# Hybrid decoder step on one core: 14 of 17 tiles of h reach the router through a DRAM round trip and VectorE's 32x32 transposes

## Chip, core and metric

One core of one Trainium2 chip runs one launch of the kernel. The metric is the time of that launch on the device in microseconds (us), lower is better. All arrays are float32. Engines are named as the profile names them: PE is TensorE (PEld its weight loads), DVE is VectorE, ACT is ScalarE, POOL is GpSimd, SP is SyncE, here the engine that issues most DMAs.

## What is computed

One decoder layer for 2048 prompt tokens and 8 sample tokens, model width 1024:

```python
proj = x @ w_in + b_in                      # attention and convolution halves side by side
attn = window_attention(rope(q), rope(k), v)   # window 128, 8 heads, 2 kv heads
conv = silu(layer_norm(depthwise_conv(ca * sigmoid(cg)))) 
mix  = concat(attn, conv) @ w_out + b_out
h    = layer_norm(ALPHA * x + mix)          # (2056, 1024)
lg, le = h @ w_rg, h @ w_re                 # router: 4 groups, 32 experts
# top-1 group, top-2 experts in it, gates; every token goes to 2 SwiGLU experts
y    = layer_norm(ALPHA * h + moe(h))
```

The change concerns only how `h` is brought into the layout in which the router's product `h @ [w_rg, w_re]` reads it: model dimension on partitions, tokens on columns.

## The kernel before

The program has five stages: the input projection of the convolution half; attention with the rest of the input projection; the **output sweep**; the expert loop; the final LayerNorm. Each engine has its own instruction stream, and the streams meet at semaphores (`after(engine, sem, c)` waits for the count c + 1).

The output sweep handles one tile per step `c` = 0 to 16 (`OUT_IN`: first the sample tile of 8 rows, then the 16 prompt tiles of 128 rows). It runs as a software pipeline, and every engine has a hand-written order:

- **PE**, step c: `project_out(c, 0)` (L850, 8 products of 512 columns, the first half of h's columns), `turn_z(c+1)` (L830, four transposes of the convolution output), `router(c-2)` (L868, 8 small products of hT with the router weights), `project_out(c, 1)`, `rank(c-2)` (L875, L876), and `turn_h(c-1)` (L859): 8 transposes of 128x128, which read `r[:, k::8]` and write the PSUM tile `bank_T`.
- **ACT**: `turned_h` (L1151) copies `bank_T` into `hT` in SBUF, one instruction, and raises `hT_ev`. `router(c)` waits for `hT_ev`; it also waits for `rk_ev`, which DVE's `route_count` of the tile before raises.
- **DVE**, step c: `route_count(c-3)` and `route_slot(c-3)` (L1554 to L1564), `conv_stats(c+2)` (L1450, waits for the tile of `conv_rows`), `gain_conv(c+1)` (L1458), `add_half(c, 0)` (L1483), `route_top(c-2)` (L1507 to L1534), `mix_conv(c+1)` (L1466), `route_gate(c-2)` (L1540 to L1549), `add_half(c, 1)` (L1483, raises `o1_ev`), `norm_h(c)` (L1490 to L1495).
- **POOL and ACT** finish h (`rstd_h`, `scale_h`, `bias_h`), which raises `h_ok`.
- **SP**, step c: `load_conv(c+2)` (L503), `store_h(c-1)` (L528 to `h_rows`, L529 to `sum_rows`, 512 KB each), `load_attn(c+2)` (L512, waits for PE's second half), `load_x(c+2)` (L522, waits for `o1_ev` of c), and for c = 1 to 9 `load_matrix` (L489): 1 MB of expert weights each, ahead of the expert loop.

`h` is stored to DRAM (`h_rows`) for every tile in any case, since the expert loop gathers its rows from there. `hT` has one buffer (the old `ptA`); `ptB` (`flat_ptB`) is free during the sweep.

Of the kernel before, what the change touches and what calls it, by code (L numbers as in the profile page):

```python
# [14 lines left out]
P = 128  # L15
# [142 lines left out]
pe_o0 pe_o1 o0_ev o1_ev lstat_ok lrs_ok dg_ok lz_ok h_ok h_out0 h_out1 pe_hT hT_ev pe_ro ro_ev ro_nm ro_e1 ro_d ro_e2  # L158
oh_ok pe_rk rk_ev slot_ok sc_out0 sc_out1 last_out s_cache s_row s_vs
pe_sA sA_ev pe_sB pe_sC sm_ok s_exp s_p pe_sD sD_ev pe_sF s_fin sconv_ok pe_sN sN_ev  # L160
# [6 lines left out]
def layer(nc, a, o, scratch):  # L167
    with ExitStack() as ctx:
# [198 lines left out]
        OUT = [PAIR[0]] + [PAIR[c % 2 == 0] for c in range(1, NT + 1)]  # L367
        CHUNK_OF = [(0, 1), (2, 3)] + [(step + 2,) for step in range(2, CHUNKS - 2)]
# [30 lines left out]
        def _(sp):  # L399
# [130 lines left out]

            for step in range(STEPS):
# [8 lines left out]
                if step == 2:  # L540
                    sp.wait_ge(s["pe_sA"], 1)
# [14 lines left out]
                if step == 3:  # L556
                    sp.dma_start(ln_g, a["ln1_g"].partition_broadcast(P)).then_inc(s["ln1_in"], 16)
                    sp.wait_ge(s["pe_sB"], 1)
                    sp.dma_start(ln_b, a["ln1_b"].partition_broadcast(P)).then_inc(s["ln1_in"], 16)
# [27 lines left out]
            for c in range(NT + 1):  # L587
                if 1 <= c <= NT - 2:
                    load_conv(c + 2)
                if c >= 1:  # L590
                    store_h(c - 1)
                if c + 2 <= NT:
                    if c >= 1:
                        load_attn(c + 2)
                    load_x(c + 2)
                if 1 <= c <= 3 * (WR - 1):
                    if c == 4:
                        sp.wait_ge(s["cvd_st1"], 64)
                    load_matrix(0, 1 + (c - 1) // 3, (c - 1) % 3)
            store_h(NT)  # L600
# [47 lines left out]
        def _(pe):  # L648
# [126 lines left out]
            def sample_piece(step):  # L775
                if step == 1:
# [15 lines left out]
                    last.then_inc(s["pe_sA"], 1)  # L792
                elif step == 2:
# [7 lines left out]
                    last.then_inc(s["pe_sB"], 1)  # L801
                elif step == 3:
                    pe.wait_ge(s["sA_ev"], 2)
                    tr(M0[0:64, 128:256], sT, ident).then_inc(s["pe_sC"], 1)
                elif step == 4:
                    pe.wait_ge(s["s_p"], 1)
                    tr(M0[:, 128:192], Ps, ident[0:64, 0:64]).then_inc(s["pe_sD"], 1)
                elif step == 5:
# [5 lines left out]
                    last.then_inc(s["pe_sF"], 1)  # L814
                elif step == 6:
# [3 lines left out]
                    last.then_inc(s["pe_sN"], 1)  # L819
# [131 lines left out]
            for c in range(1, NT + 3):  # L951
# [12 lines left out]
                if 0 <= c - 1 <= NT:  # L964
                    turn_h(c - 1)
# [91 lines left out]
        def _(act):  # L1057
# [32 lines left out]
            def sample_piece(step):  # L1090
                if step == 1:
                    act.wait_ge(s["pe_sA"], 1)
# [7 lines left out]
                elif step == 2:  # L1100
                    act.wait_ge(s["pe_sB"], 1)
# [8 lines left out]
                elif step == 4:  # L1110
                    act.wait_ge(s["pe_sD"], 1)
                    fn(PTs, M0[:, 128:192], ACT.Copy).then_inc(s["sD_ev"], 1)
                elif step == 5:
                    act.wait_ge(s["pe_sF"], 1)
# [3 lines left out]
                elif step == 6:  # L1118
                    act.wait_ge(s["pe_sN"], 1)
                    fn(cn[0][0:DEC, :], M0[0:DEC, :], ACT.Copy).then_inc(s["sN_ev"], 1)  # L1120
# [26 lines left out]
            def turned_h(c):  # L1147
                n = rows_of(OUT_IN[c])
                after(act, s["pe_hT"], c)
# [40 lines left out]
            for c in range(NT + 3):  # L1190
# [8 lines left out]
                if 0 <= c - 1 <= NT:  # L1199
# [110 lines left out]
        def _(v):  # L1310
# [116 lines left out]
            def sample_max():  # L1427
                v.wait_ge(s["pe_sC"], 1)
# [39 lines left out]
            def add_half(c, half):  # L1468
                n, b = rows_of(OUT_IN[c]), c % 2
                cols = slice(512 * half, 512 * (half + 1))  # L1470
                if half == 0:
# [3 lines left out]
                    if c >= 2:  # L1475
                        after(v, s["pe_hT"], c - 2)
# [9 lines left out]
            def norm_h(c):  # L1486
# [8 lines left out]
                stt(r[b][0:n, :], r[b][0:n, :], lmv[0:n, 0:1], ln_g[0:n, :], ALU.subtract, ALU.mult).then_inc(s["dg_ok"], 1)  # L1495

# [69 lines left out]
            for step in range(STEPS):  # L1566
# [8 lines left out]
                if I:  # L1575
# [9 lines left out]
                    if step == 1:  # L1585
                        v.wait_ge(s["pe_sA"], 1)
# [34 lines left out]
            for c in range(NT + 4):  # L1621
                if 0 <= c - 3 < NT - 1:
# [339 lines left out]
```

## Time and profile before

| | us |
|---|---|
| median of 3 runs | 1447.11 |
| lowest and highest | 1442.04, 1457.03 |
| the profiled execution | 1445.06 |
| its span in the profile | 1443.2 |

The mean granted clock of TensorE over the span is 0.955 of full speed. The output sweep lies between about 579 and 880 us of the span. In the profile's timeline each row has a start, a length, an engine, a line, an operation, its output and inputs, and in brackets how long the engine had been idle before it and what released it. A matmul in float32 shows as two records.

### The profile page before, as it was taken

The page shows a single profiled execution, that of the slowest core. Times are in us where ns is not written, and L with a number is a line of the kernel's source. Part 1 is how long each engine was busy: PE and PEld are TensorE (multiplying, and loading weights), DVE is VectorE, ACT ScalarE, POOL GpSimd, SP SyncE. Part 2 cuts the span into 40 slices and gives each one's busy share as a digit, 9 for nine tenths or more (in the row PEclk, how much of TensorE's full clock was granted, in tenths as well). Part 3 has the DMA queues.
Part 4 walks back from the last instruction along what each step waited for, and adds up shares of the span by engine and source line. Part 5 has one row for each costly group of instructions (what it writes and reads, how often), then busy time and mean ns, then how long its engine had stood idle before and what let it go on. Part 6 is the DMA issues. An engine that isn't in the chain of part 4 may idle for free.

```text
span 1443.2 us, 20676 instructions
## 1 busy us (share of the span) xinstructions
PE 1306.3 (91%) x5827; PEld 647.7 (45%) x5828; DVE 578.1 (40%) x1787; ACT 593.5 (41%) x883; POOL 382.2 (26%) x530
## 2 busy tenths in 40 slices
PE   8999998989999988999999994999999999999800
PEld 3444435656666654455555552333333333333300
DVE  2424243635655545476676653111111111111168
ACT  0001002434445434143333321666666666666455
POOL 5113110000000001455555542123333333333134
PEclk9999999999999989999999995999999999999955
DMA  6364533222112373344553313469799888998684
GB/s 249 113 221 146 175 109 116 64 88 67 60 58 74 107 236 122 119 175 175 175 178 131 123 59 118 135 204 345 198 339 345 271 282 261 348 329 274 178 294 189
DMA packets 83135, 261.55 MB, mean 181 GB/s; under 512 B 15384, under 2 KB 34080, under 8 KB 69894
## 3 DMA queue, kind: packets, MB, share of 16 engines
q1 hardware_dynamic: 62775, 216.26, 41.6%
q0 software_dynamic: 12320, 40.93, 12.2%
q10 hardware_dynamic: 7959, 3.43, 1.0%
q8 instruction: 32, 0.52, 0.2%
q14 instruction: 49, 0.40, 0.1%
HBM read 202.04 MB, written 62.78 MB: 183 GB/s over the span
## 4 chain that ended last, share of the span: by engine, by line
PE 58%; issue 28%; DMA 6%; DVE 3%; ACT 2%; POOL 1%; SPq 1%; POOLq 1%; ACTq 1%; DVEq 1%
PE P L1003 12%; PE bank_S L1027 9%; PE M L1003 6%; PE bank_S L850 6%; PE P L850 5%; PE bank_S L677 4%; PE P L677 3%; PE bank_T L985 2%; PE bank_T L677 2%; PE M L677 2%; DMA work<-conv_rows 2%; PE M L868 2%; DMA big<-in_w 1%; PE M L1013 1%; DMA big<-sum_rows 1%
## 5 line engine op out<-in xcount | busy, mean ns | idle before, releaser
L1003 PE MATMUL P<-big,work 128*64 x416 | 187.0, 603 | 2.6 <-ACT work L1217 2.4
L1004 PE MATMUL P<-big,work 128*64 128x512 f32 x416 | 187.1, 603 | 0.0
L716 PE MATMUL P<-big,work 128*128 128x256 f32 (+1 forms) x512 | 173.7, 496 | 0.0
L1245 ACT ACTIVATE big<-big 128x2048 f32 x78 | 144.8, 1902 | 30.2 <-issue 16.4
L1027 PE MATMUL bank_S<-big,work 128*64 x312 | 143.6, 603 | 3.7 <-ACT big L1251 3.0
L1029 PE MATMUL bank_S<-big,work 128*64 128x512 f32 x312 | 143.6, 603 | 0.0
L716 PEld LDWEIGHTS P<-big,work 128*128 128x128 f32 x512 | 97.3, 194 | 70.4 <-issue 63.6
L850 PE MATMUL P<-big,work 128*128 128x512 f32 x256 | 116.2, 608 | 2.7 <-DVE work L1483 2.7
L1698 DVE COPY work<-M 128x256 f32<-128x256 f32 x39 | 16.6, 424 | 254.6 <-PE M L1013 254.6
L850 PE MATMUL bank_S<-big,work 128*128 128x512 f32 x256 | 113.3, 595 | 0.0
L1003 PEld LDWEIGHTS P<-big,work 128*64 128x64 f32 x416 | 55.5, 138 | 126.4 <-issue 126.4
L1805 POOL TENSOR_TENSOR tick<-tick 1x1 f32<-1x1 f32 x192 | 31.8, 183 | 269.8 <-DMA tab<-slot_rows 171.3
L1817 POOL TENSOR_SCALAR work<-work 128x1 f32<-128x1 f32 (+1 forms) x17 | 3.8, 222 | 373.2 <-DVE work L1452 373.2
L1003 PE MATMUL M<-big,work 128*64 x208 | 92.0, 595 | 2.4 <-ACT big L1245 2.3
L1004 PE MATMUL M<-big,work 128*64 128x512 f32 x208 | 92.0, 595 | 0.0
L1074 ACT ACTIVATE work<-work 128x512 f32<-128x512 f32 (+1 forms) x17 | 10.7, 630 | 176.1 <-DVE work L1352 133.8
L1703 DVE TENSOR_SCALAR work<-bank_S,tab 128x512 f32<-128x512 f32 x39 | 29.3, 751 | 133.1 <-PE bank_S L1029 126.5
L1086 ACT ACTIVATE work<-work 128x256 f32<-128x256 f32 x128 | 63.4, 496 | 40.8 <-DVE work L1389 40.8
L850 PEld LDWEIGHTS P<-big,work 128*128 128x128 f32 x256 | 48.5, 195 | 58.4 <-issue 55.5
L1251 ACT ACTIVATE big<-big 128x2048 f32 x39 | 74.0, 1897 | 0.6 <-issue 0.6
L1027 PEld LDWEIGHTS bank_S<-big,work 128*64 128x64 f32 x312 | 39.9, 138 | 76.4 <-issue 71.9
L850 PEld LDWEIGHTS bank_S<-big,work 128*128 128x128 f32 x256 | 47.4, 190 | 53.7 <-issue 53.6
(301 smaller groups left out, 2307.6 us busy)
## 6 DMA issues: line engine op xcount, KB each, us to landing
big<-in_w SPq DMA_DIRECT2D x96, 1024.0 KB, 11.8
work<-in_xt_prompt SPq DMA_DIRECT2D x32, 512.0 KB, 3.7
big<-in_toe SPq DMA_DIRECT2D x16, 512.0 KB, 3.4
work<-in_x_prompt SPq DMA_DIRECT2D x16, 512.0 KB, 4.2
h_rows<-work SPq DMA_DIRECT2D x16, 512.0 KB, 2.7
sum_rows<-work SPq DMA_DIRECT2D x16, 512.0 KB, 3.7
big<-sum_rows SPq DMA_DIRECT2D x16, 512.0 KB, 9.1
out_y_prompt<-big SPq DMA_DIRECT2D x16, 512.0 KB
```

What stands on the lines that cost most here:

```text
L677: last = mm(dst, lhs[:, k, :], rhs[:, k, :], start=(first and k == 0), stop=(final and k == KD // 2 - 1), skip_group_check=not first)
L716: last = mm(dst[0:n, 0:c1 - c0], lhs[:, k, :], w_qkv[:, k, c0:c1], start=(k == 0), stop=(k == KD - 1))
L850: last = mm(OUT[c][half][0:n, :], lhs[:, k, :], w_out[:, k, half * 512:(half + 1) * 512], start=(k == 0), stop=(k == KD - 1))
L1003: mm(lower, xgT[:, k, 0:U], both[:, k], start=(k == 0), stop=(k == KD - 1))
L1004: last = mm(upper, xgT[:, k, U:P], w_up[:, k], start=(k == 0), stop=(k == KD - 1))
L1027: mm(bank_S[0:U, cols], gT[:, k, 0:U], wmem[:, bass.ds(off + 2 * KD * FF + k * D + half * 512, 512)], start=(k == 0), stop=(k == 1))
L1029: last = mm(bank_S[U:P, cols], gT[:, k, U:P], w_dn[:, k, cols], start=(k == 0), stop=(k == 1))
L1086: fn(smx[:, i, :], smx[:, i, :], ACT.Exp, bias=nm[:, c0 + i:c0 + i + 1], scale=SCALE, accum_out=rs[:, c0 + i:c0 + i + 1])
L1245: fn(w_up.rearrange("p k m f -> p m k f")[:, :, ks, :], src, ACT.Copy).then_inc(s[f"wu{part}_ok"], 1)
L1251: fn(big[:, 2 * KD * FF:WCOLS], wmem[:, bass.ds(off + 2 * KD * FF, 2 * D)], ACT.Copy).then_inc(s["wd_ok"], 1)
L1703: ts(ye[:, j * D + 512:(j + 1) * D], bank_S[:, 512:], tab[:, j6, 1:2], None, ALU.mult).then_inc(s["y_ev1"], 1)
L1805: gtt(tick[:, col[0]:col[0] + 1], tick[:, 0:1], tick[:, 0:1], ALU.add)
```

## The change

For 14 of the 17 tiles (all but those of c = 0, 15 and 16, `BY_PE`) `turn_h` on PE and `turned_h` on ACT are left out. In their place SP reads the tile back from `h_rows` in four DMAs, each into 32 partitions: partition 32j + t gets columns 256j to 256j+255 of rows t, 32+t, 64+t and 96+t, so 128 runs of 1 KB in each DMA. DVE then turns all 32x32 blocks with one instruction of 128x1024, which writes `hT` and raises `hT_ev`. SP issues `reload_h(c-1)` at the end of its step c, behind `load_x` and `load_matrix`; DVE runs `flip_h(c-2)` at the start of its step c, ahead of `route_count(c-3)`. Besides, seven semaphores of the sample tile are merged into one (`pe_smp`), which makes room for `hp_in`.

```diff
+        BY_PE = (0, NT - 1, NT)
+        h_parts = flat_ptB
@@ SP
+            def reload_h(c):
+                tile = OUT_IN[c]
+                sp.wait_ge(s[f"h_out{c % 2}"], 32 * (c // 2 + 1))
+                after(sp, s["hT_ev"], c - 1)
+                src = h_dram[P * tile:P * (tile + 1), :].rearrange("(i t) c -> t i c", t=32)
+                for j in range(4):
+                    sp.dma_start(h_parts[32 * j:32 * (j + 1), :].rearrange("p (i c) -> p i c", i=4),
+                                 src[:, :, 256 * j:256 * (j + 1)]).then_inc(s["hp_in"], 16)
...
                     load_matrix(0, 1 + (c - 1) // 3, (c - 1) % 3)
+                if c >= 1 and c - 1 not in BY_PE:
+                    reload_h(c - 1)
@@ PE
-                if 0 <= c - 1 <= NT:
+                if c - 1 in BY_PE:
                     turn_h(c - 1)
@@ ACT
-                after(act, s["pe_hT"], c)
+                after(act, s["pe_hT"], BY_PE.index(c))
...
-                if 0 <= c - 1 <= NT:
+                if c - 1 in BY_PE:
                     turned_h(c - 1)
@@ DVE
-                        after(v, s["pe_hT"], c - 2)
+                        after(v, s["pe_hT"], sum(x <= c - 2 for x in BY_PE) - 1)
                         v.wait_ge(s[f"h_out{b}"], 32 * (c // 2))
...
+            def flip_h(c):
+                v.wait_ge(s["hp_in"], 64 * c)
+                after(v, s["pe_ro"], c - 1)
+                nc.vector.transpose(hT.rearrange("p k (i t) -> p i k t", i=4),
+                                    h_parts.rearrange("p (i f k) -> p i k f", i=4, k=KD)).then_inc(s["hT_ev"], 1)
...
             for c in range(NT + 4):
+                if 0 <= c - 2 < NT and c - 2 not in BY_PE:
+                    flip_h(c - 2)
                 if 0 <= c - 3 < NT - 1:
```

## Rows read from the trace of the kernel before

**Rows 1.** Page: span; busy time of each engine.

```profile
span 1443.2 us, 20676 instructions
PE 1306.3 (91%) x5827; PEld 647.7 (45%) x5828; DVE 578.1 (40%) x1787; ACT 593.5 (41%) x883; POOL 382.2 (26%) x530
```

**Rows 2.** Windows: engines' busy time, granted clock, DMA share, GB/s.

```profile
655.00:675.00 20.00, 20.00 (x72) 10.83 (x71) 12.42 (x50) 7.81 (x10) 10.49 (x12) 1.00 0.54 191
```

**Rows 3.** Timeline of PE, 640 to 680 us.

```profile
642.48 1.87 PE L868 MATMUL M<-wr,work 128*128 128x36 f32 x16
...
651.50 1.13 PE L859 MATMUL bank_T<-const,work 128*128 128x128 f32 x8
652.46 7.03 PE L850 MATMUL P<-big,work 128*128 128x512 f32 x16
...
659.76 1.87 PE L868 MATMUL M<-wr,work 128*128 128x36 f32 x16
```

**Rows 4.** Timeline of SP's queue and DVE over one step with a matrix.

```profile
652.05 0.33 SPq L522 DMA_DIRECT2D work<-in_x_prompt  x1
...
652.48 0.38 SPq L489 DMA_DIRECT2D big<-in_w  x1
...
652.97 0.36 SPq L503 DMA_DIRECT2D work<-conv_rows  x1
...
653.78 1.28 DVE L1495 SCALAR_TENSOR_TENSOR work<-work,lnx 128x1024 f32<-128x1024 f32 x1
...
654.99 0.18 DVE L1554 TENSOR_TENSOR route<-M,counts 128x32 f32<-128x32 f32 x1
...
655.93 0.16 DVE L1564 SCALAR_TENSOR_TENSOR slot_i<-work 128x2 int32<-128x2 f32 x1
...
660.50 0.69 DVE L1450 BATCH_NORM_STATS2 work<-work 128x6 f32<-128x512 f32 x1 [4.41 <-DMA work<-conv_rows]
...
668.87 0.68 DVE L1483 SCALAR_TENSOR_TENSOR work<-work,P 128x512 f32<-128x512 f32 x1
...
669.58 0.33 SPq L522 DMA_DIRECT2D work<-in_x_prompt  x1
```

**Rows 5.** Timeline of SP's queue: `load_x` of steps 2 and 10.

```profile
618.39 0.33 SPq L522 DMA_DIRECT2D work<-in_x_prompt  x1
...
756.79 0.33 SPq L522 DMA_DIRECT2D work<-in_x_prompt  x1
```

**Rows 6.** DMA issues, 640 to 760 us: count, KB, us to landing.

```profile
big<-in_w SPq DMA_DIRECT2D x6, 1024.0 KB, 6.9
...
work<-conv_rows SPq DMA_DIRECT2D x7, 256.0 KB, 7.5
```

**Rows 7.** DMA issues, 760 to 830 us, steps without a matrix.

```profile
work<-in_x_prompt SPq DMA_DIRECT2D x4, 512.0 KB, 4.2
work<-conv_rows SPq DMA_DIRECT2D x3, 256.0 KB, 4.4
```

**Rows 8.** Timeline of a step without a matrix: `load_x` and the router.

```profile
791.35 0.33 SPq L522 DMA_DIRECT2D work<-in_x_prompt  x1
...
798.95 1.86 PEld L868 LDWEIGHTS M<-wr,work 128*128 128x128 f32 x16
```

**Rows 9.** Windows while `gather_windows` (1 KB runs, 32 partitions) lands.

```profile
106.00:107.00 1.00, 1.00 (x4) 0.42 (x3) 0.00 (x0) 0.00 (x0) 0.00 (x0) 1.00 1.07 263
107.00:108.00 1.00, 1.00 (x4) 0.38 (x3) 0.23 (x1) 0.00 (x0) 0.00 (x0) 1.00 0.94 193
```

**Rows 10.** Timeline of PE: work after two idle stretches.

```profile
579.07 10.14 PE L850 MATMUL P<-big,work 128*128 128x512 f32 x16 [2.72 <-DVE work L1483]
...
1367.38 1.11 PE L1027 MATMUL bank_S<-big,work 128*64 x1 [3.04 <-ACT big L1251]
```

**Rows 11.** Windows: granted clock (third number from the end) after these stretches.

```profile
580.00:582.00 2.00, 2.00 (x4) 0.88 (x3) 1.81 (x4) 0.00 (x0) 2.00 (x2) 0.50 0.00 0
...
1370.00:1372.00 2.00, 2.00 (x12) 0.67 (x8) 0.00 (x0) 0.00 (x0) 0.00 (x0) 0.95 0.50 98
```

More of the change, by code:

```diff
@@ L157 @@
 cn_in0 cn_in1 am_in0 am_in1 xr_in0 xr_in1 xb_ok cstat_ok cnm_ok z_ev pe_z zl_ok zs_ok mix_ok
-pe_o0 pe_o1 o0_ev o1_ev lstat_ok lrs_ok dg_ok lz_ok h_ok h_out0 h_out1 pe_hT hT_ev pe_ro ro_ev ro_nm ro_e1 ro_d ro_e2
+pe_o0 pe_o1 o0_ev o1_ev lstat_ok lrs_ok dg_ok lz_ok h_ok h_out0 h_out1 hp_in pe_hT hT_ev pe_ro ro_ev ro_nm ro_e1 ro_d ro_e2
 oh_ok pe_rk rk_ev slot_ok sc_out0 sc_out1 last_out s_cache s_row s_vs
-pe_sA sA_ev pe_sB pe_sC sm_ok s_exp s_p pe_sD sD_ev pe_sF s_fin sconv_ok pe_sN sN_ev
+pe_smp sA_ev sm_ok s_exp s_p sD_ev s_fin sconv_ok sN_ev
 early_out tab_build pe_tab eids_ok idx_ok tab_in0 tab_in1 tab_in2 tab_in3 tab_in4 tab_in5
@@ L791, in sample_piece @@
                                       ident[0:NROW, 0:NROW])
-                    last.then_inc(s["pe_sA"], 1)
+                    last.then_inc(s["pe_smp"], 1)
                 elif step == 2:
@@ L813, in sample_piece @@
                                   PTs[:, b * HEADS:(b + 1) * HEADS], start=True, stop=True)
-                    last.then_inc(s["pe_sF"], 1)
+                    last.then_inc(s["pe_smp"], 1)
                 elif step == 6:
@@ L818, in sample_piece @@
                         last = tr(M0[0:DEC, c * P:(c + 1) * P], conv_s[:, c, :], ident)
-                    last.then_inc(s["pe_sN"], 1)
+                    last.then_inc(s["pe_smp"], 1)
                 elif step == 9:
@@ L1091, in sample_piece @@
                 if step == 1:
-                    act.wait_ge(s["pe_sA"], 1)
+                    act.wait_ge(s["pe_smp"], 1)
                     for c in range(CC):
@@ L1100, in sample_piece @@
                 elif step == 2:
-                    act.wait_ge(s["pe_sB"], 1)
+                    act.wait_ge(s["pe_smp"], 2)
                     sT4 = view(sT, b=DEC, kv=KVH, g=G)
@@ L1110, in sample_piece @@
                 elif step == 4:
-                    act.wait_ge(s["pe_sD"], 1)
+                    act.wait_ge(s["pe_smp"], 4)
                     fn(PTs, M0[:, 128:192], ACT.Copy).then_inc(s["sD_ev"], 1)
                 elif step == 5:
-                    act.wait_ge(s["pe_sF"], 1)
+                    act.wait_ge(s["pe_smp"], 5)
                     o_v = M0[:, 256:256 + 64].rearrange("p (b kv g) -> p kv g b", b=DEC, kv=KVH)
@@ L1118, in sample_piece @@
                 elif step == 6:
-                    act.wait_ge(s["pe_sN"], 1)
+                    act.wait_ge(s["pe_smp"], 6)
                     fn(cn[0][0:DEC, :], M0[0:DEC, :], ACT.Copy).then_inc(s["sN_ev"], 1)
@@ L1427, in sample_max @@
             def sample_max():
-                v.wait_ge(s["pe_sC"], 1)
+                v.wait_ge(s["pe_smp"], 3)
                 nc.vector.tensor_reduce(s_mx, M0[0:64, 128:256], AX, ALU.max)
@@ L1585, in _ @@
                     if step == 1:
-                        v.wait_ge(s["pe_sA"], 1)
+                        v.wait_ge(s["pe_smp"], 1)
                     if S:
```

10 lines of the change are left out of this document (5 added, 5 removed).

## The prediction

> **What bounds the kernel now.** I read the page first. PE is busy 91% of the span [rows 1], so work taken off PE looks like time won. Then I read the windows of 20 us over the output sweep. In the one that stands here for them PE has no idle time at all, at a granted clock of 1.00 [rows 2]: in this stage, too, PE looks like the bound. DVE is busy 12.4 of 20 us, ACT 7.8, the DMA engines 54%. The timeline of PE gives the period, from one router (642.48) to the next (659.76), 17.28 us, and what the transposes take of it, from 651.50 to the start of the next `project_out`, 652.46: 0.96 us [rows 3].
>
> The timeline of SP and DVE shows a second loop beside PE's, and the reader should see that it is as long. Starting where `o1_ev` lets SP go (652.05): `load_x`, `load_matrix` (652.48), `load_conv` (652.97), then DVE sits idle 4.41 us until conv_rows have landed and goes on at 660.50. It works almost without a pause until `add_half(c, 1)` at 668.87, which lets the next `load_x` go at 669.58: 17.53 us [rows 4]. So the steps with a matrix are tied by a transfer as well as by PE. The reason for the long wait is in the DMA groups: conv_rows take 7.5 us to land when 1 MB of weights is queued ahead of them and 4.4 us when it is not [rows 6, 7]. What is queued behind the matrix waits for it. The change puts its read-back exactly there.
>
> **The change part by part.**
>
> *Removed.* 14 x 0.96 = 13.4 us of PE [rows 3] and the copies on ACT. ACT is idle for more than half of the stage [rows 2], so its part counts as nothing. The 13.4 us are the gain if nothing else grows. The merged semaphores cost nothing: their waits are those of before, in the same places.
>
> *Added on SP.* Four DMA issues a tile, each about as long as that of L503, 0.36 us [rows 4], so some 1.6 us. They push `load_conv` back by as much; `store_h` comes 6 us later and has room. The waits of `reload_h` (h stored, hT of the tile before turned) were met a period ago.
>
> *Added on the DMA queue.* 0.52 MB between the matrix and conv_rows. The matrix has landed 6.9 us after 652.48, at 659.4 [rows 4, 6]. What 0.52 MB in runs of 1 KB into 32 partitions take is shown by the windows in which the same form (`gather_windows`) lands with the engines fully busy: 193 to 263 GB/s [rows 9], that is 2.0 to 2.7 us. The lower bound is the matrix's own rate of 333 GB/s, 1.6 us. (1.05 MB in the 3.15 us between the landing of x, 652.05 + 4.2, and its own [rows 4, 6, 7].) I take 2.1 us, so the read-back is complete at 661.5 (661.0 to 662.1).
>
> The Trainium skill (SBUF — State Buffer, Door 1: The DMA port swizzle) says that a transfer to 32 partitions reaches only half of the SBUF ports, and so half of the rate of some 435 GB/s. By it the estimate would be 2.4 us, 0.3 us more in each step; the trace's windows agree in kind.
>
> *Added on DVE.* One instruction of 128x1024. No transpose of DVE is in the trace. The nearest row of its size takes 1.28 us [rows 4]. Bounds: 0.69 us, a row of half the columns, if it ran at double rate [rows 4]; 2.6 us, twice the nearest row, if it read in two passes or paid for its stride of 8 elements. I take 1.28, since it too moves 1024 elements of each partition. The Trainium skill (Vector Engine (DVE) Microarchitecture Reference, section 3.8 The reshape front-end and per-opcode configuration) says that the transpose sustains an element per cycle and lane; from 0.96 GHz that is an estimate of 1.07 us, 0.2 us less per tile.
>
> *The wait it adds.* `flip_h` stands first in DVE's step and blocks it until the read-back has landed. Behind it are `route_count` and `route_slot`, 654.99 to 656.09 = 1.1 us, which lay in idle time before [rows 4], and `rk_ev`, for which the router waits too (about 0.45 us after the turn, a term as long as the two counting instructions).
>
> **Steps with a matrix** (read-backs of steps 2 to 9, eight of them), in the times of [rows 3, 4], `o1_ev` at 652.05:
> - The turn ends at 661.5 + 1.28 = 662.8, the router starts at 663.25. PE, freed of the transposes, is ready for it at 659.76 - 0.96 = 658.8, so it idles 4.4 us.
> - From the router to the next `load_x` PE needs 652.05 - 642.48 = 9.55 us: 672.8, a loop of 20.8 us.
> - DVE's own chain: 662.8 + 1.1 + (668.87 - 660.50 = 8.4) + 0.7 = 673.0, a loop of 20.9. Both agree.
> - The clock. After an idle stretch of 2.72 us the granted clock is 0.50 (1.2 GHz), and one half of `project_out` takes 10.14 us where it takes 7.03, a loss of 3.1 [rows 3, 10, 11]. After 3.04 us of idling it is low too, and back before 1370.1, 2.6 us into the work, a loss of 1.3 [rows 10, 11]. 4.4 us is longer than both. I take the mean, 2.2 us a step, on PE's chain: 20.8 + 2.2 = 23.0 us.
>
> Eight steps took 756.79 - 618.39 = 138.4 us [rows 5]; they will take 8 x 23.0 = 184.0: **+45.6 us**.
>
> **Steps without a matrix** (six, steps 10 to 15): x lands at 791.35 + 4.2 = 795.55 [rows 7, 8], the read-back 2.1 later, the turn ends at 798.9, the router starts at 799.4 where it started at 798.95 [rows 8]. The 0.96 us are used up and 0.45 more: 6 x 0.45 = +2.7 us. Bounds: 796.5 for the landing (conv_rows landed so soon after x: 791.79 + 4.4 is 796.2 [rows 7, 8]; its issue is 0.44 after that of `load_x`) and 0.69 for the turn leave PE's gain whole, -5.8 us; 798.25 and 2.6 give +14 us.
>
> Sum: +48.3 us against 1445.06 of the profiled execution, 1493.4. The median shown lies 2.05 above that execution, so 1495.
>
> **The rivals.**
> 1. *As forecast, but the clock holds* (or falls for moments only). For it: two stretches are few cases, and the work ahead of them was other work. Against it: both stretches of [rows 10] are shorter than 4.4 us. Without the clock's term the loop is 20.9: 8 x 20.9 - 138.4 = +28.8, with 2.7 in all +31.5: 1478.6. With both low bounds (661.0, 0.69) DVE's chain is 19.8 us and the sum is +20 - 5.8: 1461.
> 2. *The transfers are hidden: faster.* The turn of tile c is needed only after half a `project_out` and `turn_z` of the next step, 658.8. If the read-back did not queue behind the matrix but shared the engines with it, and landed by 657.1, which is 4.1 us after the matrix's issue slot at 652.97, the router would never wait and the whole 13.4 us would be won: 1447.1 - 13.4 = 1433.7. The place is SP's queue, the price is the landing, and the point from which it decides is 4.1 us for the landing, or 5.4 us for landing and turn together, counted from 652.97. Against it stands conv_rows' 7.5 us in the same slot with half the bytes [rows 6].
> 3. *No change to speak of.* The read-back lands between, at about 659, so that the router starts at 660.75 and the loop is 18.3 us (8 x 18.3 - 138.4 = +8), and the steps without a matrix gain or lose a little: 1448 to 1460. It needs the matrix to give way by some 2.5 us; nothing in the rows shows that.
> 4. *Worse than forecast.* The router's small products run at the low clock as well before it recovers, 1.7 us more in each of eight steps, or the turn costs 2.6 us: 8 x 1.7 or 8 x 1.3 + 6 x 1.3, and in the latter case the idle stretch of the steps without a matrix grows to some 2.8 us, so the clock falls there too, 6 x 2.2. That gives 1509 to 1528.
>
> **How the numbers follow.** Forecast 0.50 (1480 to 1508 with its own bounds), rival 1 0.20, rival 4 0.18, rival 2 0.05, rival 3 0.07. The range 1462 to 1532 leaves out rivals 2 and 3 and the tail of rival 4. 1% of 1447 is 14.5 us, about what a measurement of this kernel can tell from no change. Over it on the slow side: 0.88; within it 0.07; faster 0.05.
>
> **What would show each step.** Right: L859 has 24 transposes left; DVE's idle time before the turn is released by the DMA from h_rows, about 6 us in steps with a matrix; PE waits about 4 us before L868 in eight steps and under 1 us in six; the granted clock falls below 1.00 between 620 and 800 us; `load_x` comes every 23 us up to step 10 and every 17.5 us after. Wrong: a read-back that lands in under 5 us behind the matrix, a turn of over 2 us, or a clock of 1.00 in spite of 4 us of idling. If PE waits for the DVE's counting instead of the turn, the forecast's size may hold but its step would be another.

## The result and the profile after

The median went from 1444.61 to 1547.29 us (the kernel before beside it on the same chip). The ratio is 1.069, with an interval of 1.062 to 1.076: slower by 6.9%. The direction held, and so did the mechanism in the steps with a matrix. The size did not: +48 us were forecast and +103 came, and 1547 lies outside the range of 1462 to 1532. In the steps without a matrix a loss came that the prediction had left out. The profiled execution of after has a span of 1548.7 us against 1443.2 [rows 1].

Where the 105.5 us lie, by the issues of `load_x` and of the first list load of the expert loop:

| stretch | before | after | more | forecast |
|---|---|---|---|---|
| steps 2 to 10 (matrix in each) | 138.4 | 215.0 | 76.6 | 45.6 |
| steps 10 to 14 | 69.1 | 89.1 | 20.0 | 1.8 (4 x 0.45) |
| step 14 to the expert loop | 60.4 | 66.3 | 5.9 | 0.9 |
| all else | | | 3.0 | 0 |

The page of after shows less work on PE's transposes but more busy time of PE, because it works at a lower clock. The last line here is the granted clock in 40 slices of the span. The nine slices of 8 and 7 from 619 to 968 us are the output sweep. The single 5 behind them stands in the page of before too.

```profile
span 1548.7 us, 20508 instructions
...
PE 1342.1 (87%) x5715; PEld 664.0 (43%) x5716; DVE 608.7 (39%) x1801; ACT 578.8 (37%) x869; POOL 381.6 (25%) x530
...
PEclk9999999999999899888788888599999999999955
```

The waits of after from 640 to 830 us (us in total, times, longest):

```profile
DVE work L1513 <- DMA work<-h_rows: 57.7, 7, 9.6
...
PE M L881 <- DVE counts L1575: 47.6, 7, 8.1
...
DVE work L1496 <- PE P L863: 14.5, 4, 4.0
```

DVE waits for the read-back in each of the seven steps of the stretch, 8.2 us at a time, and PE waits 6.8 us on average (5.9 to 8.1) before the router. The last line shows the loop closing: DVE waits for PE's slow `project_out` before the `add_half` that lets the next `load_x` go.

One step, in the timeline of SP, PE and DVE. It is the counterpart of [rows 3, 4]; L524 is `load_x`, L491 `load_matrix`, L539 the read-back, L505 `load_conv`, L1513 the turn, L881 the router, L863 `project_out`.

```profile
723.15 0.33 SPq L524 DMA_DIRECT2D work<-in_x_prompt  x1
...
723.53 0.43 SPq L491 DMA_DIRECT2D big<-in_w  x1
...
724.05 2.72 SPq L539 DMA_DIRECT2D work<-h_rows  x4
...
726.89 0.59 SPq L505 DMA_DIRECT2D work<-conv_rows  x1
...
735.00 2.01 DVE L1513 STREAM_TRANSPOSE work<-work 128x1024 f32<-128x1024 f32 x1 [8.83 <-DMA work<-h_rows]
...
737.49 3.60 PE L881 MATMUL M<-wr,work 128*128 128x36 f32 x16 [7.34 <-DVE counts L1575]
...
740.89 9.20 PE L863 MATMUL P<-big,work 128*128 128x512 f32 x16
...
750.13 0.69 DVE L1496 SCALAR_TENSOR_TENSOR work<-work,P 128x512 f32<-128x512 f32 x1 [3.50 <-PE P L863]
```

Count from `load_x` at 723.15. The turn starts at 11.85, the router at 14.34, and the next `add_half(c, 1)` ends at 750.82, so the loop is 27.7 us long. The router's 16 small products take 3.60 us where they took 1.87, and half of `project_out` takes 9.20 where it took 7.03 [rows 3]. The windows of the same step (busy PE, PEld, DVE, ACT, POOL; granted clock, DMA share, GB/s) say why:

```profile
732.00:734.00 2.00, 0.00 (x0) 0.00 (x0) 0.00 (x0) 0.00 (x0) 0.00 (x0) 1.00 1.07 273
742.00:744.00 2.00, 2.00 (x4) 0.90 (x3) 1.53 (x8) 1.97 (x3) 1.82 (x2) 0.50 0.01 4
744.00:746.00 2.00, 2.00 (x4) 0.72 (x3) 1.55 (x7) 1.22 (x4) 1.20 (x2) 0.72 0.01 1
746.00:748.00 2.00, 2.00 (x6) 0.95 (x5) 0.47 (x4) 0.00 (x0) 0.00 (x0) 1.00 0.05 5
```

While PE idles, the DMA engines are full. The matrix has landed by 732.0; what moves in the window at 732 is the rest of the read-back and the two stores of h, which SP issues at 730.29 and 730.67. Then PE works at a granted clock of 0.50 (1.2 GHz) until about 745 and has 1.00 again in the window at 746.

The DMA issues of 640 to 800 us (count, KB, us from issue to landing). The matrix takes 8.6 us where it took 6.9, conv_rows 8.3 where they took 7.5 [rows 6]:

```profile
big<-in_w SPq DMA_DIRECT2D x6, 1024.0 KB, 8.6
...
work<-h_rows SPq DMA_DIRECT2D x24, 128.0 KB, 7.8
...
work<-conv_rows SPq DMA_DIRECT2D x6, 256.0 KB, 8.3
```

The means over steps 3 to 9 and over the four periods from step 10 give the table that the rest of the document works with. All are us after `load_x`; "router to load_x" is PE's own chain from the router's first product to the next issue of `load_x`.

| | period | turn starts | turn | router to load_x |
|---|---|---|---|---|
| with matrix, forecast | 23.0 | 9.45 | 1.28 | 11.75 |
| with matrix, measured | 27.27 | 11.31 | 2.01 | 13.47 |
| without, forecast | 17.7 | 6.3 | 1.28 | 9.55 |
| without, measured | 22.27 | 7.62 | 2.01 | 12.16 |

So three terms are too small: the time at which the read-back has landed, the turn and the clock. The experiments take them one at a time.

### The profile page after: what moved, and what is told of

Same layout as the page of the kernel before. It is cut to its first block, busy times and chain, and to the rows that moved or that the text cites. A ratio compares the mean times of both kernels' runs of the same rounds, so it can differ in the third digit from the quotient of the medians.

```text
span 1548.7 us, 20508 instructions
## 1 busy us (share of the span) xinstructions
PE 1342.1 (87%) x5715; PEld 664.0 (43%) x5716; DVE 608.7 (39%) x1801; ACT 578.8 (37%) x869; POOL 381.6 (25%) x530
## 4 chain that ended last, share of the span: by engine, by line
PE 52%; issue 26%; DMA 11%; DVE 4%; SPq 2%; ACT 2%; POOL 1%; ACTq 1%; POOLq 1%; DVEq 0%
PE P L1016 10%; PE bank_S L1040 8%; DMA work<-h_rows 6%; PE M L1016 6%; PE bank_S L863 4%; PE P L863 4%; PE bank_S L690 3%; PE M L881 3%; PE P L690 3%; PE bank_T L998 2%; PE bank_T L690 2%; PE M L690 2%; DMA big<-in_w 2%; DVE work L1513 2%; SPq L539 1%
## 5 line engine op out<-in xcount | busy, mean ns | idle before, releaser
L1258 ACT ACTIVATE big<-big 128x2048 f32 x78 | 144.8, 1902 | 33.2 <-issue 20.2
L863 PE MATMUL P<-big,work 128*128 128x512 f32 x256 | 131.0, 671 | 3.3 <-DVE work L1496 3.3
L729 PEld LDWEIGHTS P<-big,work 128*128 128x128 f32 x512 | 97.4, 194 | 70.4 <-issue 63.6
L863 PE MATMUL bank_S<-big,work 128*128 128x512 f32 x256 | 127.0, 653 | 0.0
L881 PE MATMUL M<-wr,work 128*128 128x36 f32 (+1 forms) x272 | 51.3, 363 | 72.0 <-DVE counts L1575 72.0
L863 PEld LDWEIGHTS P<-big,work 128*128 128x128 f32 x256 | 54.3, 218 | 67.7 <-issue 64.2
L881 PEld LDWEIGHTS M<-wr,work 128*128 128x128 f32 (+1 forms) x272 | 49.6, 282 | 75.6 <-DVE work L1513 71.1
L863 PEld LDWEIGHTS bank_S<-big,work 128*128 128x128 f32 x256 | 52.8, 212 | 61.7 <-issue 61.6
```

The costliest lines, as they stand in the source:

```text
L729: last = mm(dst[0:n, 0:c1 - c0], lhs[:, k, :], w_qkv[:, k, c0:c1], start=(k == 0), stop=(k == KD - 1))
L863: last = mm(OUT[c][half][0:n, :], lhs[:, k, :], w_out[:, k, half * 512:(half + 1) * 512], start=(k == 0), stop=(k == KD - 1))
L881: last = mm(M0[0:n, 0:NG + NE], hT[:, k, 0:n], wr_v[:, k, :], start=(k == 0), stop=(k == KD - 1))
L1258: fn(w_up.rearrange("p k m f -> p m k f")[:, :, ks, :], src, ACT.Copy).then_inc(s[f"wu{part}_ok"], 1)
```

## The experiments

Theory A, from the prediction: the read-back queues behind the matrix, `flip_h` blocks DVE, the router comes late, and after the pause PE works at the low clock. Its rivals: the turn on DVE is itself the burden (B), the transfer costs by its bytes wherever it stands (C), and the stores of h wait for or share the queue with it (D).

### 1. The turn alone, with no transfer

```diff
-                if c >= 1 and c - 1 not in BY_PE:
-                    reload_h(c - 1)
...
-                v.wait_ge(s["hp_in"], 64 * c)
+                after(v, s["h_ok"], c)
...
-                ... h_parts.rearrange("p (i f k) -> p i k f", i=4, k=KD) ...
+                ... r[c % 2].rearrange("p (i f k) -> p i k f", i=4, k=KD) ...
```

> The changed kernel without the read-back: no DMA, DVE turns 32x32 blocks straight from r. hT then holds h in a permuted order, so the router picks other experts and the expert loop may be some us longer or shorter; the sweep is what is read. Theory A (the read-back is the cause; the 2.0 us of the turn on DVE lie in its idle time): steps of 16.3 to 17.5 us, the sweep 5 to 13 us shorter than before the change, some 1435 to 1445 us in all. Rival B (the turn on DVE itself, ahead of the counting and the conv statistics, costs the path): steps of 18.5 us or more, 1465 us or more.

Measured: 1459.88, ratio 1.009 (1.006 to 1.012). In the sweep it is faster than the kernel before: steps 2 to 10 take 137.7 us (138.4), the period without a matrix is 16.74 (17.28). What makes the total longer lies behind the sweep: h is permuted, so other experts are chosen, and the expert loop works off 41 blocks where it had 39. It begins at 876.74, before it began at 886.32. So the turn of 2.0 us on DVE does not lengthen a step where its data are there in time. B falls.

### 2. The transfer alone, with PE still turning

The kernel before with the unused read-back in its place behind the matrix.

```diff
-        BY_PE = (0, NT - 1, NT)
+        BY_PE = tuple(range(NT + 1))
...
-                after(sp, s["hT_ev"], c - 1)
+                sp.wait_ge(s["hp_in"], 64 * (c - 1))
...
-                if c >= 1 and c - 1 not in BY_PE:
+                if 1 <= c - 1 < NT - 1:
                     reload_h(c - 1)
...
-                           ("h_out1", NT)):
+                           ("h_out1", NT), ("hp_in", 4 * (NT - 2))):
```

> The kernel before with the read-back added and used by nobody: PE and ACT turn all 17 tiles as before, SP issues the same 56 DMAs at the same places behind the matrix. It leaves out the turn on DVE and the router's wait for the read-back. By the forecast's second loop (DVE waits for conv_rows, which now stand behind matrix and read-back and land some 3.5 us later in steps with a matrix): steps of 20 to 21 us with a matrix, 17.3 without, 25 to 32 us more than the kernel before, 1472 to 1478 us. If the transfer is free for whoever doesn't wait for it: 1447 us.

Measured: 1467.88 beside 1445.3, ratio 1.014 (1.009 to 1.019), some 23 us, a little less than the 25 to 32 I had expected. In its profile steps 2 to 10 take 154.6 us, +16.2, and 69.9 from 10 to 14, +0.8; about 4 us lie ahead of the sweep and 5 in the expert loop, and I have no cause for those. The timeline shows the second loop of the prediction at work: conv_rows are pushed back, and DVE starts a step's statistics at 10.27 after `load_x` in the mean of steps 3 to 9, where it started at 8.14. The step shown here is the longest, with 12.28:

```profile
717.01 0.33 SPq L524 DMA_DIRECT2D work<-in_x_prompt  x1
...
717.92 2.38 SPq L539 DMA_DIRECT2D work<-h_rows  x4
...
720.41 0.39 SPq L505 DMA_DIRECT2D work<-conv_rows  x1
...
729.29 0.69 DVE L1463 BATCH_NORM_STATS2 work<-work 128x6 f32<-128x512 f32 x1 [8.23 <-DMA work<-conv_rows]
```

So the read-back alone, with nobody waiting for it, costs +16 of the +77 us of these eight steps. C explains a fifth. The rest needs someone who waits for the read-back.

One thing more is in this trace: the last of the four DMAs lands 9.70 us after `load_x` (mean of steps 3 to 9), near the 9.45 forecast, though form and place are those of the changed kernel, where it is 11.29. So the landing depends on more than form and place. A difference that I see on the queue is the load of the attention columns: here it goes out 3.4 us ahead of `load_x`, in the changed kernel 0.72. No run tests it.

### 3. The read-back ahead of the matrix

```diff
+                if c >= 1 and c - 1 not in BY_PE:
+                    reload_h(c - 1)
                 if 1 <= c <= 3 * (WR - 1):
                     ...
                     load_matrix(0, 1 + (c - 1) // 3, (c - 1) % 3)
-                if c >= 1 and c - 1 not in BY_PE:
-                    reload_h(c - 1)
```

> The changed kernel with one thing moved: SP issues the read-back of h ahead of the matrix of expert weights instead of behind it. Theory A (what is queued behind the matrix waits for it): the read-back lands about 7.4 us after o1_ev in the steps with a matrix as it does in those without one (11.9 us now), these steps fall from 26.9 us to about 22.5, eight of them, so about 35 us less than the changed kernel: 1512 us. Rival B (the form of the read-back, 1 KB runs into 32 partitions, or the stores that now overlap it, set its landing, not its place): the steps stay at 25 us or more and the time above 1530 us.

Measured: 1504.51, ratio 1.040 (1.034 to 1.046), 43 us less than the changed kernel. Steps 2 to 10 take 170.4 us (215.0), steps 10 to 14, which have no matrix, 87.7 (89.1). The turn starts at 7.18 instead of 11.31 (mean of steps 3 to 9):

```profile
717.13 0.33 SPq L524 DMA_DIRECT2D work<-in_x_prompt  x1
...
717.56 1.80 SPq L539 DMA_DIRECT2D work<-h_rows  x4
...
719.40 0.43 SPq L491 DMA_DIRECT2D big<-in_w  x1
...
724.10 2.01 DVE L1513 STREAM_TRANSPOSE work<-work 128x1024 f32<-128x1024 f32 x1 [3.94 <-DMA work<-h_rows]
```

A holds: the place behind the matrix costs 4.1 us. And something is left: a step is now 21.5 us with a matrix and 21.9 without, 4.1 and 4.7 more than before. That part has nothing to do with the matrix.

### 4 and 5. The form of the read-back

Two other forms of the same 0.52 MB in the same place: one DMA of 128 whole rows, and four DMAs that keep the four issues and the 1 KB runs but write all 128 partitions.

```diff
-                for j in range(4):
-                    sp.dma_start(h_parts[32 * j:32 * (j + 1), :].rearrange("p (i c) -> p i c", i=4),
-                                 src[:, :, 256 * j:256 * (j + 1)]).then_inc(s["hp_in"], 16)
+                sp.dma_start(h_parts, h_dram[P * tile:P * (tile + 1), :]).then_inc(s["hp_in"], 16)
...
-                v.wait_ge(s["hp_in"], 64 * c)
+                v.wait_ge(s["hp_in"], 16 * c)
```

> The changed kernel with the form of the read-back changed: one DMA of 128 whole rows of 4 KB, a row to a partition, in place of four into 32 partitions in runs of 1 KB; same 0.52 MB, same place behind the matrix. hT then holds h in a permuted order, so the router picks other experts; the sweep is what is read. Theory C (the form costs: 1 KB runs and 32 partitions): the turn starts about 9.5 us after o1_ev with a matrix ahead (11.1 us now in the mean of steps 3 to 9) and about 6 us without (7.4 now), steps 1.5 us shorter, sweep some 20 us shorter. Rival D (the stores of h that are issued at 7.1 us and run beside the read-back take its rate): the form changes nothing, 11 and 7.4 us.

```diff
+                for j in range(4):
+                    sp.dma_start(h_parts[:, 256 * j:256 * (j + 1)],
+                                 h_dram[P * tile:P * (tile + 1), 256 * j:256 * (j + 1)]).then_inc(s["hp_in"], 16)
```

> The changed kernel with the read-back as four DMAs of 128 partitions, 1 KB of each row (columns 256j to 256j+255 of row p to partition p): runs of 1 KB and four issues as in the change, but all 128 partitions as in e5_plain_rows. hT then holds h in a permuted order; the sweep is what is read. If the 1 KB runs and the four issues are what costs 2.0 us with a matrix ahead (turn at 11.3 us after o1_ev against 9.3 with whole rows): the turn starts at 11 us here too. If the 32 partitions of each DMA are: at about 9.3 to 9.8 us.

Measured: 1532.97, ratio 1.060 (1.056 to 1.064), for whole rows, and 1530.35 in one execution for four DMAs. Steps 2 to 10 take 196.9 and 197.7 us. The totals hold two more blocks of the expert loop, as in experiment 1, so the sweep is what compares. A step with the four DMAs, in which the turn starts 9.86 us after `load_x`:

```profile
735.18 0.33 SPq L524 DMA_DIRECT2D work<-in_x_prompt  x1
...
736.08 2.21 SPq L538 DMA_DIRECT2D work<-h_rows  x4
...
745.04 2.01 DVE L1512 STREAM_TRANSPOSE work<-work 128x1024 f32<-128x1024 f32 x1 [6.84 <-DMA work<-h_rows]
```

| form | turn starts, with matrix | without |
|---|---|---|
| four DMAs, 32 partitions each | 11.31 | 7.62 |
| one DMA, 128 partitions | 9.31 | 6.29 |
| four DMAs, 128 partitions, 1 KB runs | 9.31 | 5.46 |

With a matrix ahead the 1 KB runs and the four issues cost nothing: the two lower rows agree. (Without one the four DMAs are ahead by 0.8 us, but there x has landed after 3.3 us where it took 4.2 with whole rows, so this is not shown to be the form.) What costs 2.0 us is writing 32 partitions at a time.

The landings in the traces split these 2.0 us. The DMA issues of 640 to 800 us with whole rows:

```profile
big<-in_w SPq DMA_DIRECT2D x7, 1024.0 KB, 7.6
work<-h_rows SPq DMA_DIRECT2D x7, 512.0 KB, 8.3
```

The matrix lands 7.6 us after its issue, in the changed kernel 8.6. In the steps whose landing of the matrix is in the trace it comes, counted from `load_x`, at 8.05 with whole rows, 7.89 with four DMAs of 128 partitions and 9.26 in the changed kernel. The last of the read-back follows it by 1.24, 1.39 and 2.35 us. So writing 32 partitions makes the read-back itself some 1.1 us longer, and the matrix lands 1.2 to 1.4 us later as well. The read-back does not stand strictly behind the matrix either: in four of these five steps of the changed kernel the first of its four DMAs landed before the matrix.

The Trainium skill (SBUF — State Buffer, Door 1: The DMA port swizzle) says that 32 partitions reach half the ports. This case agrees in kind. As estimates from its figures, 0.52 MB at half of 435 GB/s take 2.4 us and at the whole rate 1.2, a difference of 1.2 us. Behind the landing of the matrix 1.0 to 1.1 were measured; the turn's start moved by 2.0 (1.3 to 2.2 without a matrix).

### 6. Do the stores take its rate?

Theory D: `store_h` of 0.52 MB is on the same queue and may slow the read-back. Here each store waits until the read-back has landed.

```diff
                 after(sp, s["h_ok"], c)
+                if c >= 2 and c - 1 not in BY_PE:
+                    sp.wait_ge(s["hp_in"], 64 * (c - 1))
                 sp.dma_start(h_dram[P * tile:P * tile + n, :], r[c % 2][0:n, :])...
```

> The changed kernel with one wait added: the two stores of a tile are issued only when the read-back before it has landed, so they no longer run beside it. Theory D (the stores take its rate): the turn starts at about 9.5 to 10 us after o1_ev with a matrix ahead (11.1 us now), and steps are 1.2 us or more shorter, 8 to 15 us less than the changed kernel. Theory C (the form of the read-back costs): still 11 us, the time within 5 us of the changed kernel's.

Measured: 1550.86, ratio 1.073 (1.069 to 1.076); steps 2 to 10 take 218.2 us. The first store now goes out 12 us after `load_x` instead of 7.1, and the turn starts at 11.94 and 8.1 all the same. Nothing is won, so D falls.

### 7. The turn's own time

The same instruction reading stride 1 instead of stride 8 (this permutes h).

```diff
-                ... h_parts.rearrange("p (i f k) -> p i k f", i=4, k=KD) ...
+                ... h_parts.rearrange("p (i k f) -> p i k f", i=4, k=KD) ...
```

> The changed kernel with one size changed: the turn on DVE reads its columns in memory order (stride 1) instead of stride 8, the written side and the number of elements are the same. hT then holds h in a permuted order, so the router picks other experts; only the length of the one instruction is read. If the stride costs: 1.1 to 1.3 us instead of 2.0. If the turn of 128x1024 float32 costs 2.0 us whatever it reads: 2.0.

The turn's line in both kernels (count, shortest/mean/longest in ns), after and then this one:

```profile
L1513 DVE STREAM_TRANSPOSE work<-work x14: 2005/2006/2029, 626.3 to 947.9; 128x1024 f32<-128x1024 f32 x14
```

```profile
L1513 DVE STREAM_TRANSPOSE work<-work x14: 1239/1245/1247, 625.2 to 932.1; 128x1024 f32<-128x1024 f32 x14
```

2.01 us with stride 8, 1.25 with stride 1: the stride costs 0.76. The whole kernel took 1556.12 us in its one execution, in spite of the shorter turn. With a matrix the turn started at 12.25 on average instead of 11.31, which took back what was won. Over the kernels in which DVE waits for the read-back in this form and place (after and experiments 6, 7 and 8) the mean is 11.3 to 12.3. The read-back's distance from the matrix is the same, 2.3 to 2.5 us; it is the matrix that lands later, at 9.77 here against 9.26. What moves the matrix I did not find. In the steps without a matrix the shorter turn shows: two of four periods are 18.0 and 18.8 us (all four were 21.2 to 23.8 in the changed kernel), the ones in which the clock did not fall.

### 8. The clock's part

PE gets something to do while it waits: unused products of 512 columns into `bank_T`, which is free there. They change no wait.

```diff
                 if c + 1 <= NT:
                     turn_z(c + 1)
+                if 0 <= c - 2 <= NT and c - 2 not in BY_PE:
+                    for k in range(7 if c <= 10 else 2):
+                        mm(bank_T[:, 0:512], w_out[:, k, 0:P], w_out[:, k, 0:512], start=True, stop=True)
```

> The changed kernel with added work on PE: products of 512 columns into the unused PSUM tile bank_T (7 of them in steps with a matrix, 2 in the others), between turn_z and the router, where PE sits idle. Their results are used by nothing. Theory A (the fall of the granted clock after the idle stretch costs 3 to 4 us a step, and DVE's own chain binds some 0.5 us later): clock 1.00 through the sweep, steps of about 23.4 us with a matrix and 19.5 without, 40 to 48 us less than the changed kernel: about 1503 us. Rival B (the low clock is hidden behind DVE's chain): no change, 1547 us, or a few us more from the added work.

Measured: 1517.56, ratio 1.049 (1.043 to 1.055): 30 us faster than the changed kernel, though PE does more. (With two executions here the 30 are uncertain by some 14 us either way; in the traces steps 2 to 14 are 27 us shorter.) The turn starts as late as ever (11.59), and PE still waits for it:

```profile
745.57 6.17 PE L971 MATMUL bank_T<-big 128*128 128x512 f32 x14
...
753.13 1.95 PE L881 MATMUL M<-wr,work 128*128 128x36 f32 x16 [1.38 <-DVE counts L1578]
...
754.91 7.11 PE L863 MATMUL bank_S<-big,work 128*128 128x512 f32 x16
```

The router takes 1.95 us (3.60) and `project_out` 7.11 (9.20). From the router to `load_x`, steps 3 to 9: 11.34, 9.64, 9.57, 11.33, 9.64, 11.34, 9.65; in the changed kernel 12.7 to 13.8. So the low clock costs 3.9 us in such a step of the changed kernel (13.47 on average against 9.6), and the part of it that the filler takes away is about 30 of the 103 us. I had expected 40 to 48. In three of seven steps, and in three of the four periods without a matrix, the granted clock still fell. The length of the wait that is left does not tell which: in these eleven steps it fell behind waits of 1.26, 1.27, 1.32, 1.64, 1.70 and even 0.76 us before the router, and held behind 0.80, 1.38 and 1.53. What decides it the runs do not show. The values stand in groups, 9.6, 11.3 and 13.0: an extra of 0, 1.7 or 3.4 us.

### 9. The read-back behind its own store

If A is right, the place is the fault. Here the read-back of a tile is issued right behind its store, when the queue holds little, and has half a step, some 8.6 us, before the turn that needs it.

```diff
                     store_h(c - 1)
+                if c >= 1 and c - 1 not in BY_PE:
+                    reload_h(c - 1)
...
                     load_matrix(0, 1 + (c - 1) // 3, (c - 1) % 3)
-                if c >= 1 and c - 1 not in BY_PE:
-                    reload_h(c - 1)
```

> The changed kernel with one thing moved: SP issues the read-back right behind the store of the same tile (it waits there for the store to land), half a step earlier than now, when the queue is empty and before the attention columns, x and the matrix of the next step are issued. Theory A (only the place of the read-back is at fault): it has landed before DVE reaches the turn, PE does not idle, the clock stays at 1.00; the steps with a matrix stay bound by conv_rows behind the matrix (17.5 us), those without fall to 16.4: 1436 to 1444 us, 0 to 8 us less than the kernel before. Rival B (SP, held up by the wait, issues the attention columns and x too late): steps of 18 to 20 us, 1455 to 1490 us.

Measured: 1440.19, ratio 0.9945 (0.992 to 0.997): 107 us less than the changed kernel, by the place of four issues. Steps 2 to 10 take 137.8 us, steps 10 to 14 67.0; the clock is 1.00 and the turn starts at 2.9 with no wait. The period without a matrix is 16.75, not 16.4, though, and the timeline shows why (this step has a matrix; in one without, the custom instruction at 795.75 takes 1.99):

```profile
723.30 0.35 SPq L524 DMA_DIRECT2D work<-in_x_prompt  x1
...
726.24 2.03 DVE L1513 STREAM_TRANSPOSE work<-work 128x1024 f32<-128x1024 f32 x1
...
728.07 2.35 POOL L1870 TENSOR_TENSOR work<-work,lnx 128x1024 f32<-128x1024 f32 x1 [1.32 <-ACT work L1151]
...
728.52 1.95 DVE L1579 CUSTOM_DVE_ANT_0 route<-work,route 128x32 f32<-128x32 f32 x1
...
734.83 1.74 SPq L539 DMA_DIRECT2D work<-h_rows  x4
```

The small custom instruction of `route_slot` (L1579) takes 1.95 us where it takes 0.18 to 0.19 elsewhere. It starts at 728.52 and ends at 730.47; POOL's `bias_h` ends at 730.42. The turn ahead of it pushed it into POOL's instruction. The same happens in experiment 1, with the same period.

The Trainium skill (SBUF — State Buffer, Who interferes with whom) says that a DVE instruction with two inputs in SBUF contends with a GpSimd one that reads SBUF, while one with a single input, outside the 2-port perf modes, doesn't. The trace agrees: the custom instruction reads `work` and `route` and ends 0.05 us behind `bias_h`.

### 10. The turn behind the counting

The prediction of that reading: let the small instructions go first, and put the turn, which has one input, under `bias_h`.

```diff
-                if 0 <= c - 2 < NT and c - 2 not in BY_PE:
-                    flip_h(c - 2)
                 if 0 <= c - 3 < NT - 1:
                     route_count(c - 3)
                     route_slot(c - 3)
+                if 0 <= c - 2 < NT and c - 2 not in BY_PE:
+                    flip_h(c - 2)
```

> The read-back right behind the store, as in e4_after_store, and on DVE the turn behind route_count and route_slot instead of ahead of them. In e4 the turn pushes route_slot into POOL's bias_h, and one of its instructions then takes 1.95 us instead of 0.19; the conv statistics start 7.7 us after o1_ev and DVE sets a period of 16.75 us. Theory: with the order changed the instruction is short again, the conv statistics start at about 6 us in steps without a matrix (7.5 with one, when conv_rows have landed), PE sets the period, 16.3 to 16.5 us, 2 to 6 us less in all than e4: 1434 to 1438 us. Rival (the turn itself is then what runs into bias_h and is lengthened by as much): period unchanged, 1440 us.

Measured: 1435.55, ratio 0.992 (0.990 to 0.995). The interval overlaps that of experiment 9, so it is the steps that show the gain, not the total. The custom instruction is back at 0.18 us, and the turn beside `bias_h` takes 2.06:

```profile
791.82 0.18 DVE L1579 CUSTOM_DVE_ANT_0 route<-work,route 128x32 f32<-128x32 f32 x1
...
792.51 2.06 DVE L1513 STREAM_TRANSPOSE work<-work 128x1024 f32<-128x1024 f32 x1
...
793.29 2.37 POOL L1870 TENSOR_TENSOR work<-work,lnx 128x1024 f32<-128x1024 f32 x1 [1.32 <-ACT work L1151]
```

Steps without a matrix are now 16.4 us (16.75 in experiment 9). Those with one take 17.1 on average: DVE waits for conv_rows until 7.3 to 8.8 us after `load_x`.

### 11 and 12. conv_rows ahead of the matrix

The same cure for the other transfer behind the matrix: the kernel of experiment 10 with `load_conv` one step earlier and ahead of `load_matrix`, and that move alone in the kernel before.

```diff
-                if 1 <= c <= NT - 2:
-                    load_conv(c + 2)
...
                     load_x(c + 2)
+                if c <= NT - 3:
+                    load_conv(c + 3)
                 if 1 <= c <= 3 * (WR - 1):
```

> The kernel of e8_turn_behind_count with the load of conv_rows issued ahead of the matrix instead of behind it. There the conv statistics wait for conv_rows until 7.3 to 8.8 us after o1_ev in the steps with a matrix (mean period 17.1 us) and start at 6.0 in those without (16.4). Theory (the last wait of these steps is conv_rows' place in the queue): all steps at 16.4 us, 5 to 6 us less than e8: about 1430 us. Rival (the matrix is late then, or x and conv_rows share the rate): periods stay at 17, 1435 us.

> The kernel before (all 17 tiles turned by PE and ACT, no read-back) with the one move of e11_conv_first alone: conv_rows are loaded ahead of the matrix. If the gain of e11 (ratio 0.989 to the kernel before) comes from the turns leaving PE: this kernel stays bound by PE at 17.28 us a step, and since its steps with a matrix took 17.3 us in the mean it is the same as before, 1443 to 1448 us. If the gain comes from the move of conv_rows alone: about 1430 us.

Measured: 1430.34 beside 1445.3, ratio 0.989 (0.986 to 0.993), the fastest of all; and 1442.99 beside 1444.56, ratio 0.998 (0.996 to 1.001), no difference. One step of the first:

```profile
694.30 0.35 SPq L524 DMA_DIRECT2D work<-in_x_prompt  x1
...
694.76 0.36 SPq L505 DMA_DIRECT2D work<-conv_rows  x1
...
695.17 0.43 SPq L491 DMA_DIRECT2D big<-in_w  x1
...
698.28 2.06 DVE L1513 STREAM_TRANSPOSE work<-work 128x1024 f32<-128x1024 f32 x1
...
705.44 1.75 SPq L539 DMA_DIRECT2D work<-h_rows  x4
...
710.71 0.35 SPq L524 DMA_DIRECT2D work<-in_x_prompt  x1
```

The turn at 698.28 waits for nothing; the read-back for the next one goes out at 705.44, ahead of the next `load_x` at 710.71, and so ahead of all bulk. The period is 16.4 us in every step from step 3 on. The windows of 640 to 830 us, of this kernel and then of the kernel before:

```profile
640.00:830.00 190.00, 190.00 (x643) 100.25 (x642) 153.94 (x500) 64.47 (x93) 104.95 (x110) 1.00 0.58 187
```

```profile
640.00:830.00 190.00, 189.49 (x703) 104.75 (x702) 123.86 (x462) 72.71 (x99) 102.30 (x110) 1.00 0.45 157
```

PE is busy 190.00 and 189.49 of 190 us, at a granted clock of 1.00. Where PE is the bound, taking 0.96 us of transposes off it pays, as the prediction priced it; 17.28 to 16.40 is 0.88 a step. In the kernel before, the move of conv_rows gives nothing (138.2 against 138.4), because PE's own loop of 17.28 stands there. Only the two moves together show the second loop.

## Why the prediction was right in kind and half in size

**What bounds the kernel: right.** PE's loop and DVE's loop beside it, tied by what is queued behind the matrix. Experiments 2, 10, 11 and 12 show both loops: 16.4 us when both are relieved, 17.1 with conv_rows behind the matrix, 19.3 with the transfer added.

**PE's saving: right and drowned.** 0.88 us a tile, of the 0.96 forecast, once nothing else binds (experiment 11).

**The landing: the term was 1.9 us too small, outside its own bounds.** The turn started at 11.31 instead of 9.45 (bounds 8.95 to 10.05). The sum let the matrix land as before, 6.9 us after its issue, and put the read-back's 2.1 us behind that. The read-back's own term was nearly right: its last DMA landed 2.35 us behind the matrix. What failed is the 6.9: the matrix landed after 8.6. The sum had the matrix delay the read-back and nothing delay the matrix, while in the trace both are under way at once. The form has a part in it, since with 128 partitions the matrix landed after 7.6 and the read-back 1.24 later (experiment 4). The read-back alone is not enough to explain it: in experiment 2, with the same one behind it, the matrix landed after 6.4 (the two landings from 640 to 800 us that the trace has). In steps without a matrix the error was 1.3 us, and there it was x that landed after 5.5 to 6.0 us instead of 4.2.

**The turn: 2.01 us, not 1.28.** The bounds of 0.69 to 2.6 held it; the value between was wrong. The nearest row was of equal size but not of equal stride, and the dense turn of experiment 7, 1.25 us, is that row's 1.28. The stride of 8, which I put in the upper bound, costs 0.76. A turn of over 2 us was one of the prediction's own signs of being wrong.

**`rk_ev` and the counting: right.** The router starts 2.49 us after the turn's start, 0.48 after its end, where 0.45 was forecast.

**The clock with a matrix: 3.9 us, not 2.2.** I took the mean of two losses, 3.1 and 1.3, from stretches idle for 2.7 and 3.0 us [rows 10], for a wait that I put at 4.4 and that came out at 5.9 to 8.1. The term left out the router, whose 16 small products run at the low clock first: 3.60 - 1.87 = 1.7, then 9.20 - 7.03 = 2.2, together 3.9. Rival 4 had named the router's 1.7 and given it too little.

**The clock without a matrix: 2.6 us where I had none.** This is the step of the argument that failed, not only a size. The sum had PE wait 1.4 us before the router in these steps and gave that no price in clock. With the later landing (+1.3) and the longer turn (+0.7) the wait grew to 2.9 to 3.9 us, and the clock fell in all of them. One such step:

```profile
853.79 0.33 SPq L524 DMA_DIRECT2D work<-in_x_prompt  x1
...
861.19 2.00 DVE L1513 STREAM_TRANSPOSE work<-work 128x1024 f32<-128x1024 f32 x1 [4.38 <-DMA work<-h_rows]
...
863.68 2.78 PE L881 MATMUL M<-wr,work 128*128 128x36 f32 x16 [2.89 <-DVE counts L1575]
...
866.27 9.65 PE L863 MATMUL bank_S<-big,work 128*128 128x512 f32 x16
```

Rival 4 had this chain as well, but only behind a turn of 2.6 us. Nor is it shown that 1.4 us would have been free: in experiment 5 the 1.7 us were lost behind waits of 0.74 and 1.20 us (the granted clock of 875 to 877 us is 0.59) and not behind 0.79 and 1.29.

**The sum again with the measured terms.** With a matrix: 23.0 + 1.85 (landing) + 0.73 (turn) + 1.7 (clock) = 27.3, the period measured. Without: 17.7 + 1.3 + 0.7 + 2.6 = 22.3, the period measured. Eight times 4.3 is 34, six times 4.6 is 28, and with the forecast's 48 that makes 110, against 105.5 of the trace (the last steps lose less). Of the 62 us that were missing in the sum, the clock is 29, the landing 23 and the turn 10. The range failed since it had no room for a landing above its bound, and since I kept the mishaps of rival 4 apart; but the router at the low clock and the clock lost without a matrix share a cause, the late router, and so came together.

**Open.** Why the matrix, and with it the same read-back, lands sooner in one kernel than in another (the read-back after 9.7 us in experiment 2, 11.3 to 12.3 where it is waited for); what decides whether a short wait costs the clock; whether the stretch ahead of the sweep and the expert loop of experiment 2 lost their 9 us to the queue or to something else.

## What to carry to other kernels

Put the read of a round trip through DRAM right behind its own write, not behind a bulk load that nobody awaits: the place of four issues was worth 107 us here. Price a stall with what follows it, since PE's next 1.7 to 3.9 us of loss come after its end, and behind the long stalls they begin in the smallest products. And when two unknown costs feed one wait, widen the range for both at once: together they lengthened the stall enough to lose the clock, which the forecast had kept in the steps without a matrix.

## What the runs showed of the hardware that I had not expected

- Where PE waited less than 4 us before the router, the loss came in groups of 0, 1.7 and 3.4 us (router to `load_x` 9.6, 11.3, 13.0), not in proportion to the wait: 1.7 us were lost behind a wait of 0.74 us, nothing behind one of 1.53.
- `STREAM_TRANSPOSE` of 128x1024 takes 1.25 us at stride 1 and 2.01 at stride 8, and 2.06 under a POOL instruction of 2.37 us; a custom DVE instruction of 0.18 us met the same POOL instruction and took 1.95.
- Four DMAs to 32 partitions landed 2.0 us later than four of the same bytes and runs to 128, and the 1 MB issued ahead of them landed later too (9.26 us after `load_x` against 7.89).
